# Second mixer's scan: clipped exponents, a triangle on the scores, paired gate SiLUs and a later norm root

## The chip, the cores and the metric

One core of one Trainium2 chip runs the whole program in a single launch. The metric is device time in microseconds (us), the median of several executions. All arithmetic is fp32; matmuls that need fp32 accuracy are done as three passes over split operands.

## The reference

Two blocks of two layers each on a sequence of 512 tokens with 1024 channels. The part that the change touches is the second block's second mixer, a state space mixer with 4 groups of 8 heads, cut here to what matters:

```
z, xbc, dt_raw = split(h @ w_in)
xbc = silu(causal_conv(xbc) + conv_b)
xs, b_in, c_in = split(xbc)
dt = softplus(dt_raw + dt_bias)
a_cs = cumsum(dt * a) within each chunk of 128 tokens
l_mat = exp(a_cs[t] - a_cs[s])          for s <= t, else 0
cb = c_in @ b_in^T                      scores of one chunk and group
y_diag = (cb * l_mat) @ (xs * dt)
states = b_in^T @ (xs * dt * exp(a_cs[end] - a_cs))
carry  = exp(a_cs[end]) * carry + states            over the chunks
y = y_diag + exp(a_cs) * (c_in @ carry) + xs * d
y = y * silu(z)
y = y * rsqrt(mean(y*y over the group's 512 channels) + eps) * norm_g
out = y @ w_out
```

## The kernel before

The program is written engine by engine: each engine (TensorE = PE, VectorE = DVE, ScalarE = ACT, GpSimd = POOL, SyncE = SP) has its own list of instructions in a fixed order, and they meet through counting semaphores. Nothing is scheduled by a planner; the order of the calls in `ssd_pe`, `ssd_act`, `ssd_dve`, `ssd_pool` and `ssd_sp` is the order of the work.

All projections stream their weights in slots of 256 columns: SP loads a slot (`w_raw`), ACT rounds it (`w_hi`, line 209), POOL takes the rest (`w_lo`, line 238, or line 2506 inside the scan, two instructions of 128x1024 a slot), and PE runs three matmuls per 128x128 tile (lines 248 to 250).

The scan runs 16 **slots**, v = 0 to 15, with group g = v // 4 and chunk c = v % 4. The work of one slot is spread over the engines:

- PE (`ssd_pe`): `z_half(v)`, 24 matmuls of the gate projection; `pre(v + 1)`, the transposes of x (line 2436) and the scores into `C_BANK` (line 2442); `main(v)`, per head the matmul of `lw` with `xdt` (line 2453) and, for c > 0, of `cdec` with the carried state `prev` (line 2455); then the chunk's state (line 2462). `main(v)` waits for `m_w` (DVE's product of slot v), `m_cd` (POOL's `cdec`) and `m_pv` (DVE's `states(v - 1)`).
- DVE (`ssd_dve`): `xdt` (line 2571), eight instructions of 128x128 for the exponents (line 2576), `outputs(v - 1)` (line 2548), the product of `lw` with the scores (line 2584), `states(v - 1)` (lines 2560 and 2563).
- ACT (`ssd_act`): `b_tok`, the exponentials of `cdec` (line 2486) and `lw` (line 2488), the SiLU of the gate `zT` (line 2491), and in odd slots the rounding of the next weight slot (`split_hi`). Going from one function to another costs an `ACT_TABLE_LOAD`.
- POOL (`ssd_pool`): `decay(v - 1)` of the carried state (line 2517), `xdec` (line 2528), the product for `cdec` (line 2534), and in even slots two instructions of `w_lo` (line 2506).
- SP (`ssd_sp`): `g_row` for slot v + 2 once slot v's exponents are taken (`m_dl`), the weight slots of the gate, and behind them those of `w_out`.

The norm of a finished group is laid into the next group's slots: the gating `gnorm_gate_dve` (line 2609, four of 128x512), squares on ACT (line 2615), column sums on PE (`gnorm_sums_pe`, line 2622, 8 matmuls at a time), root on ACT (`gnorm_root_act`, line 2628), reciprocal on DVE (`gnorm_rcp_dve`, line 2632), a spread over the partitions on PE (`gnorm_spread_pe`, line 2637), and the scaling on DVE (`gnorm_scale_dve`, line 2645, four of 128x512). Behind the scan `m_out_pe` starts the output projection while the last norms are finished.

The exponents before, with the mask (0 or a large negative number) as a second tensor from SBUF:

```
for k in range(8):
    op = dve.scalar_tensor_tensor(lw[v % 2][:, k, :], g_row[v % 2][:, k, :],
                                  mcols[:, M_CS, ...], upmask[:, :], ALU.subtract, ALU.add)
```

Of the kernel before, what the change touches and what calls it, by code (L numbers as in the profile page):

```python
# [26 lines left out]
P = 128  # L27
# [3 lines left out]
KD = D // P  # L31
# [75 lines left out]
def build(nc, t, out):  # L107

    ctx = ExitStack()
    with ctx:  # L110
# [2246 lines left out]
        def turn_steps_act(act):  # L2357
# [6 lines left out]
        (m_xt, m_cb, m_xd, m_dl, m_le, m_eg, m_w, m_bt, m_xe, m_cd, m_st, m_y, m_y1, m_yz, m_pd, m_pv) = (  # L2364
            sem("m_" + n) for n in "xt cb xd dl le eg w bt xe cd st y y1 yz pd pv".split())
# [47 lines left out]
        def ssd_pe(pe):  # L2413
# [50 lines left out]
            for v in range(16):  # L2464
                z_half(v)
                if v < 15:
                    pre(v + 1)
                main(v)
                if v >= 4 and v % 4 in (1, 2):
                    gnorm_sums_pe(pe, v // 4 - 1, v % 4 - 1)  # L2470
                if v >= 4 and v % 4 == 3:
                    gnorm_spread_pe(pe, v // 4 - 1)

        def ssd_act(act):
            for v in range(16):
# [63 lines left out]
        def ssd_dve(dve):  # L2539
# [25 lines left out]
            for v in range(16):  # L2565
# [9 lines left out]
                for k in range(8):  # L2575
                    op = dve.scalar_tensor_tensor(lw[v % 2][:, k, :], g_row[v % 2][:, k, :],  # L2576
                                                  mcols[:, M_CS, c * M_H + 8 * g + k:c * M_H + 8 * g + k + 1], upmask[:, :],
                                                  ALU.subtract, ALU.add)
                op.then_inc(m_dl, 1)
                if v:  # L2580
                    outputs(v - 1)
                dve.wait_ge(m_le, v + 1)
                dve.wait_ge(m_cb, v + 1)
                dve.tensor_tensor(lw[v % 2][:, :, :], lw[v % 2][:, :, :],
# [68 lines left out]
        def gnorm_act(act):  # L2653
# [363 lines left out]
```

## Time and profile before

| | us |
|---|---|
| three executions | 3088.41, 3088.75, 3091.66 (median 3088.75) |
| the profiled execution's span | 3086.1 |
| PE busy | 2914.6 (94%) |
| DVE busy | 1617.9 (52%) |
| POOL busy | 1212.1 (39%) |
| ACT busy | 1049.6 (34%) |

The span runs from the first to the last instruction of one profiled execution; its own device time is not listed apart from the three executions, which lie 2.3 to 5.6 us above that span. The profile has a page of totals, tables of busy time by stretch, a timeline of each engine with the idle time before a row and who ended it, and the mean duration of each group of instructions.

### The profile page before, as it was taken

To read this page: it belongs to the slowest core of one execution; us is meant where nothing else is said; L and a number is where in the kernel's file an instruction comes from. 1 tells how busy PE (TensorE), PEld (TensorE's weight loads), DVE (VectorE), ACT (ScalarE), POOL (GpSimd) and SP (SyncE) were. 2 spreads that over 40 slices of the span, in tenths; PEclk is the share of its full clock that TensorE was granted. 3 is DMA by queue.
4 is the path that set the end of the run, shared out by engine and by line. 5 is a ranking of instruction groups with operands and counts; after the bars stand their busy time and mean duration, and the time that the engine had idled before them with its cause. 6 is when DMAs were issued, how large, how long until landed. Compare 5 with 4: busy or idle time off the path is not lost.

```text
span 3086.1 us, 38851 instructions
## 1 busy us (share of the span) xinstructions
PE 2914.6 (94%) x14565; PEld 2374.3 (77%) x14565; DVE 1617.9 (52%) x2275; ACT 1049.6 (34%) x1327; POOL 1212.1 (39%) x556
## 2 busy tenths in 40 slices
PE   7999999999999999999998799999999988999998
PEld 6867886788877856788886677788878776778887
DVE  4435554776868146564556635555354766232224
ACT  4341122434332245333333222222235554232222
POOL 3433422344444410344443114444434544534443
PEclk9998998999999999999998779999999998999999
DMA  4320001334532320355533733655322322223322
GB/s 137 95 72 14 1 1 28 109 115 129 152 111 94 109 69 28 123 177 164 191 120 119 234 88 128 213 191 164 97 82 85 115 89 69 69 87 100 99 96 68
DMA packets 343961, 326.44 MB, mean 106 GB/s; under 512 B 28816, under 2 KB 320144, under 8 KB 343696
## 3 DMA queue, kind: packets, MB, share of 16 engines
q1 hardware_dynamic: 309760, 257.34, 26.9%
q10 hardware_dynamic: 34064, 67.18, 6.2%
q8 instruction: 97, 1.59, 0.2%
q14 instruction: 40, 0.33, 0.0%
HBM read 303.44 MB, written 21.04 MB: 105 GB/s over the span
## 4 chain that ended last, share of the span: by engine, by line
PE 72%; DVE 7%; issue 3%; ACT 2%; DMA 0%; POOL 0%; ACTq 0%; DVEq 0%; SPq 0%; POOLq 0%
PE bank L248 18%; PE bank L250 18%; PE bank L249 18%; PE bank L260 3%; PE bank L265 3%; PE bank L261 3%; PE bank L1328 2%; DVE lw L2576 1%; PE bank L1346 1%; PE bank L1336 1%; PE bank L1901 1%; PE bank L1896 1%; PE bank L2622 1%; PE bank L361 0%; DVE xt L404 0%
## 5 line engine op out<-in xcount | busy, mean ns | idle before, releaser
L238 POOL TENSOR_TENSOR w_lo<-w_raw,w_hi 128x1024 fp32r<-128x1024 f32 x400 | 1006.9, 2539 | 1446.0 <-ACT w_hi L209 1430.4
L248 PE MATMUL bank<-x_hi,w_hi 128*128 128x512 f32 x2032 | 799.5, 393 | 12.8 <-POOL w_lo L238 7.5
L250 PE MATMUL bank<-x_hi,w_lo 128*128 128x512 f32 x2032 | 793.3, 390 | 0.0
L249 PE MATMUL bank<-x_lo,w_hi 128*128 128x512 f32 x2032 | 793.1, 390 | 0.0
L209 ACT ACTIVATE w_hi<-w_raw 128x2048 fp32r<-128x2048 f32 x208 | 398.0, 1914 | 893.5 <-PE bank L250 787.5
L248 PEld LDWEIGHTS bank<-x_hi,w_hi 128*128 128x128 f32 x2032 | 383.7, 189 | 96.7 <-issue 14.9
L249 PEld LDWEIGHTS bank<-x_lo,w_hi 128*128 128x128 f32 x2032 | 383.5, 189 | 80.7 <-issue 1.6
L250 PEld LDWEIGHTS bank<-x_hi,w_lo 128*128 128x128 f32 x2032 | 382.9, 188 | 80.3
L248 PE MATMUL bank<-m_hi,w_hi 128*128 128x512 f32 x384 | 149.6, 390 | 0.0
L250 PE MATMUL bank<-m_hi,w_lo 128*128 128x512 f32 x384 | 149.4, 389 | 0.0
L249 PE MATMUL bank<-m_lo,w_hi 128*128 128x512 f32 x384 | 149.4, 389 | 0.0
L1210 DVE SCALAR_TENSOR_TENSOR y_gate<-bank,par,y_gate 128x511 f32<-128x511 f32 x88 | 66.0, 750 | 152.4 <-ACT y_gate L1144 150.7
L2209 DVE SCALAR_TENSOR_TENSOR h<-bank,mod,h 128x512 f32<-128x512 f32 (+1 forms) x64 | 47.4, 749 | 182.8 <-PE bank L250 165.7
L2188 DVE SCALAR_TENSOR_TENSOR m_r<-bank,m_r 128x512 f32<-128x512 f32 x64 | 43.8, 684 | 181.2 <-ACT m_r L2141 181.2
L1060 DVE SCALAR_TENSOR_TENSOR ada_acc<-ada_w,cond,ada_acc 128x1024 f32<-128x1024 f32 (+1 forms) x84 | 119.7, 1425 | 1.6
L2192 DVE TENSOR_TENSOR m_lo<-m_r,m_hi 128x512 fp32r<-128x512 f32 (+1 forms) x64 | 78.9, 1233 | 52.2 <-ACT m_hi L2143 52.2
L248 PE MATMUL bank<-act_hi,w_hi 128*128 128x512 f32 x264 | 103.2, 391 | 0.0
L250 PE MATMUL bank<-act_hi,w_lo 128*128 128x512 f32 x264 | 102.8, 389 | 0.0
L249 PE MATMUL bank<-act_lo,w_hi 128*128 128x512 f32 x264 | 102.7, 389 | 0.0
L260 PE MATMUL bank<-x_hi,w_hi 128*128 128x512 f32 x176 | 78.9, 448 | 18.3 <-ACT x_hi L373 7.0
L572 DVE SCALAR_TENSOR_TENSOR qkvz<-bank,par,qkvz 128x511 f32 (+2 forms) x72 | 53.8, 748 | 77.4 <-ACT qkvz L542 67.8
L836 POOL TENSOR_TENSOR X<-Rm,lev 128x512 f32<-128x512 f32 x56 | 70.3, 1270 | 54.4 <-PE bank L782 47.8
(437 smaller groups left out, 4762.1 us busy)
## 6 DMA issues: line engine op xcount, KB each, us to landing
w_raw<-in_mlp_w SPq DMA_DIRECT2D x128, 512.0 KB, 4.5
ada_w<-in_ada_w ACTq DMA_DIRECT2D x96, 512.0 KB, 4.9
w_raw<-in_f_w_up SPq DMA_DIRECT2D x88, 512.0 KB, 5.1
w_raw<-in_m_w_in SPq DMA_DIRECT2D x40, 512.0 KB, 4.7
w_raw<-in_a_w_in SPq DMA_DIRECT2D x32, 512.0 KB, 4.7
w_raw<-in_f_w_down SPq DMA_DIRECT2D x32, 512.0 KB, 4.0
w_raw<-in_w_kv SPq DMA_DIRECT2D x16, 512.0 KB, 4.3
w_raw<-in_s_w_glu SPq DMA_DIRECT2D x16, 512.0 KB, 5.3
```

The lines of the kernel that those rows point to most:

```text
L209: act.activation(w_hi[s][:, :], w_raw[s][:, :], ACT.Copy).then_inc(hi_done, 1)
L238: op = pool.tensor_tensor(w_lo[s][:, part], w_raw[s][:, part], w_hi[s][:, part].bitcast(F32), ALU.subtract)
L248: pe.matmul(dst, hi_l, hi_r, start=start, stop=False)
L249: pe.matmul(dst, hi_l, lo_r, start=False, stop=False)
L250: return pe.matmul(dst, lo_l, hi_r, start=False, stop=stop)
L260: pe.matmul(bank[o][:, :], w_hi[0][:, cols[o]], rhs_hi[:, k, :], start=(k == 0), stop=False)
L261: pe.matmul(bank[o][:, :], w_lo[0][:, cols[o]], rhs_hi[:, k, :], start=False, stop=False)
L265: mm = pe.matmul(bank[o][:, :], w_hi[0][:, cols[o]], rhs_lo[:, k, :], start=False, stop=(k == kt - 1))
L836: pool.tensor_tensor(X2[s][:, :, :], Rm[s][:, :, :], bc4(lev[:, l, :]), ALU.mult).then_inc(da_mask, 1)
L1060: dve.scalar_tensor_tensor(acc, ada_w[k][:, :, :], cond[:, k:k + 1], acc, ALU.mult, ALU.add).then_inc(ada_used, 1)
L1210: dve.scalar_tensor_tensor(y[:, s, d:T], bank[2 * s + o][:, 0:T - d], pcol("f_conv", i + (3 * 44 * f + 44 * (2 - d) + col + F_START[c] + s ...
L2192: dve.tensor_tensor(lo, m_r[:, o, :], m_hi[:, ds(2 * i + (2 * s + o), 1), :].bitcast(F32), ALU.subtract).then_inc(p_lo, 1)
```

## The change

1. The eight exponents of a slot no longer add the mask. They subtract and then clip at zero with `tensor_scalar`, which has one tensor operand. What the mask did is done on the scores: one new DVE instruction multiplies the 128x128 scores in PSUM by the 0/1 triangle `triu`, behind the waits for `m_le` and `m_cb`, and the product waits for it (`m_tri`).
2. ACT takes the gate's SiLU for slots v - 1 and v together, in odd slots.
3. The group norm is laid later: sums in the third and fourth slot of the next group (before: second and third), the root at the end of the first slot of the group after that (before: the fourth slot), the reciprocal in its second slot, the spread there ahead of `main(v)`, the scaling behind the states of that slot. For group 2 the root, the reciprocal and the spread move behind the scan, the spread between the first matmuls of the output projection.

```diff
--- before.py
+++ after.py
@@ -2361,8 +2361,8 @@
             act.dma_start(g_all, g_turn[:, :]).then_inc(m_gt, 16)
 
 
-        (m_xt, m_cb, m_xd, m_dl, m_le, m_eg, m_w, m_bt, m_xe, m_cd, m_st, m_y, m_y1, m_yz, m_pd, m_pv) = (
-            sem("m_" + n) for n in "xt cb xd dl le eg w bt xe cd st y y1 yz pd pv".split())
+        (m_xt, m_cb, m_xd, m_dl, m_le, m_eg, m_w, m_bt, m_xe, m_cd, m_st, m_y, m_y1, m_yz, m_pd, m_pv, m_tri) = (
+            sem("m_" + n) for n in "xt cb xd dl le eg w bt xe cd st y y1 yz pd pv tri".split())
         X_BANK, C_BANK, Y_BANK, N_BANK, S_BANK = bank[2], (bank[3], bank[7]), bank[4], bank[5], bank[6]
 
         def v8(x):
@@ -2465,11 +2465,11 @@
                 z_half(v)
                 if v < 15:
                     pre(v + 1)
+                if v >= 8 and v % 4 == 1:
+                    gnorm_spread_pe(pe, v // 4 - 2)
                 main(v)
-                if v >= 4 and v % 4 in (1, 2):
-                    gnorm_sums_pe(pe, v // 4 - 1, v % 4 - 1)
-                if v >= 4 and v % 4 == 3:
-                    gnorm_spread_pe(pe, v // 4 - 1)
+                if v >= 4 and v % 4 >= 2:
+                    gnorm_sums_pe(pe, v // 4 - 1, v % 4 - 2)
 
         def ssd_act(act):
             for v in range(16):
@@ -2486,16 +2486,17 @@
                     act.activation(cdec[e % 2][:, :, :], g_row[v % 2][:, :, :], ACT.Exp).then_inc(m_eg, 1)
                 act.wait_ge(m_dl, v + 1)
                 act.activation(lw[v % 2][:, :, :], lw[v % 2][:, :, :], ACT.Exp).then_inc(m_le, 1)
-                act.wait_ge(gemm_ready, 2 * z_slot(0) + v + 1)
-                ge(act, m_yz, v - 3)
-                act.activation(zT[:, v % 4, :], bank[v % 2][:, :], ACT.Silu).then_inc(bank_free, 1)
                 if v % 2:
+                    for z in (v - 1, v):
+                        act.wait_ge(gemm_ready, 2 * z_slot(0) + z + 1)
+                        ge(act, m_yz, z - 3)
+                        act.activation(zT[:, z % 4, :], bank[z % 2][:, :], ACT.Silu).then_inc(bank_free, 1)
                     n = z_slot(v // 2 + 2)
                     split_hi(act, n, n % 2, landed(n - n % 2))
                 if g and c in (1, 2):
                     gnorm_squares_act(act, g - 1, c - 1)
-                if g and c == 3:
-                    gnorm_root_act(act, g - 1)
+                if g >= 2 and c == 0:
+                    gnorm_root_act(act, g - 2)
 
         def pool_slot(pool, n):
 
@@ -2573,25 +2574,29 @@
                                   ALU.mult).then_inc(m_xd, 1)
                 dve.wait_ge(g_in[v % 2], 16 * (v // 2 + 1))
                 for k in range(8):
-                    op = dve.scalar_tensor_tensor(lw[v % 2][:, k, :], g_row[v % 2][:, k, :],
-                                                  mcols[:, M_CS, c * M_H + 8 * g + k:c * M_H + 8 * g + k + 1], upmask[:, :],
-                                                  ALU.subtract, ALU.add)
+                    op = dve.tensor_scalar(lw[v % 2][:, k, :], g_row[v % 2][:, k, :],
+                                           mcols[:, M_CS, c * M_H + 8 * g + k:c * M_H + 8 * g + k + 1], 0.0,
+                                           ALU.subtract, ALU.min)
                 op.then_inc(m_dl, 1)
                 if v:
                     outputs(v - 1)
+                if g >= 2 and c == 1:
+                    gnorm_rcp_dve(dve, g - 2)
                 dve.wait_ge(m_le, v + 1)
                 dve.wait_ge(m_cb, v + 1)
+                scores = C_BANK[v % 2][:, P:2 * P]
+                dve.tensor_tensor(scores, scores, triu[:, :], ALU.mult).then_inc(m_tri, 1)
+                dve.wait_ge(m_tri, v + 1)
                 dve.tensor_tensor(lw[v % 2][:, :, :], lw[v % 2][:, :, :],
                                   C_BANK[v % 2][:, P:2 * P].unsqueeze(1).to_broadcast([P, 8, P]), ALU.mult).then_inc(m_w, 1)
                 if v:
                     states(v - 1)
-                if v >= 4 and c == 0:
-                    if g >= 2:
-                        gnorm_scale_dve(dve, g - 2)
+                if g and c == 0:
                     gnorm_gate_dve(dve, g - 1)
-                if g and c == 3:
-                    gnorm_rcp_dve(dve, g - 1)
+                if g >= 2 and c == 1:
+                    gnorm_scale_dve(dve, g - 2)
             outputs(15)
+            gnorm_rcp_dve(dve, 2)
             gnorm_gate_dve(dve, 3)
             gnorm_scale_dve(dve, 2)
             gnorm_rcp_dve(dve, 3)
@@ -2651,6 +2656,7 @@
                 act.activation(y_hi[:, j, :], xbc[:, j, :], ACT.Copy).then_inc(hn_hi, 1)
 
         def gnorm_act(act):
+            gnorm_root_act(act, 2)
             act.wait_ge(gemm_ready, 2 * SLOTS["m_out"])
             gnorm_hi_act(act, 0, 8)
             gnorm_squares_act(act, 3, 0)
@@ -2703,10 +2709,13 @@
                         mm.then_inc(gemm_ready, 1)
             pe.wait_ge(lo_done, base + 1)
             pe.wait_ge(bank_free, 2 * base)
-            for k in range(4):
+            for k in range(2):
+                first_pair(0, k)
+            gnorm_spread_pe(pe, 2)
+            for k in range(2, 6):
                 first_pair(0, k)
             gnorm_sums_pe(pe, 3, 0)
-            for k in range(4, KD):
+            for k in range(6, KD):
                 first_pair(0, k)
             gnorm_sums_pe(pe, 3, 1)
             pe.wait_ge(lo_done, base + 2)
```

DVE around slots 8 and 9, from the reciprocal that stood at the end of slot 7. `xdt_164` and `lw_160` are the buffers of even slots, `xdt_165` and `lw_161` those of odd ones. Before:

```order
L2632 RECIPROCAL ncol<-ncol 128x4
L2571 TENSOR_TENSOR xdt_164<-bank,mcols 128x512
L2576 SCALAR_TENSOR_TENSOR lw_160<-g_row_158,mcols,upmask 128x128 x8
L2548 SCALAR_TENSOR_TENSOR xbc<-xbc,par,bank 128x128 x4
L2584 TENSOR_TENSOR lw_160<-lw_160,bank 128x1024
L2645 SCALAR_TENSOR_TENSOR xbc<-xbc,par,bank 128x512 x4
L2609 SCALAR_TENSOR_TENSOR xbc<-xbc,zT 128x512 x4
L2571 TENSOR_TENSOR xdt_165<-bank,mcols 128x512
```

After the change, the same two slots of DVE and the head of slot 10:

```order
L2572 TENSOR_TENSOR xdt_164<-bank,mcols 128x512
L2577 TENSOR_SCALAR lw_160<-g_row_158,mcols 128x128 x8
L2549 SCALAR_TENSOR_TENSOR xbc<-xbc,par,bank 128x128 x4
L2588 TENSOR_TENSOR bank<-bank,triu 128x128
L2590 TENSOR_TENSOR lw_160<-lw_160,bank 128x1024
L2614 SCALAR_TENSOR_TENSOR xbc<-xbc,zT 128x512 x4
L2572 TENSOR_TENSOR xdt_165<-bank,mcols 128x512
L2577 TENSOR_SCALAR lw_161<-g_row_159,mcols 128x128 x8
L2549 SCALAR_TENSOR_TENSOR xbc<-xbc,par,bank 128x128 x4
L2637 RECIPROCAL ncol<-ncol 128x4
L2588 TENSOR_TENSOR bank<-bank,triu 128x128
L2590 TENSOR_TENSOR lw_161<-lw_161,bank 128x1024
```

The reciprocal has left the place ahead of slot 8's `xdt` and stands in slot 9, and of the two sets of four in slot 8 only the gating is left; the scaling (line 2650) now comes behind slot 9's state copy.

PE at the end of slot 7, between `main(7)` and `z_half(8)`, as the difference of the two programs:

```order
 L2453 MATMUL bank<-lw_161,xdt_165 64x128
 L2455 MATMUL bank<-cdec_163,prev_169 64x128
-L2637 MATMUL bank<-ident,ncol 128x128 x4
+L2627 MATMUL bank<-ones,sq 128x1 x8
 L248 MATMUL bank<-x_hi,w_hi 128x512
```

The spread has left this place, and eight matmuls of sums have come to it from the slot before.

ACT in slots 9 and 10 after the change, from the table load of slot 9's exponentials:

```order
L2486 ACT_TABLE_LOAD
L2486 ACTIVATE cdec_162<-g_row_159 128x1024
L2488 ACTIVATE lw_161<-lw_161 128x1024
L2493 ACT_TABLE_LOAD
L2493 ACTIVATE zT<-bank 128x512 x2
L209 ACTIVATE w_hi<-w_raw 128x2048
L2620 ACTIVATE sq<-xbc 128x512 x2
L2481 ACTIVATE b_tok_171<-bank 128x128
```

Both SiLUs of the pair stand behind the exponential of slot 9, where each slot had one before, and the rounding and the squares come behind them as they did.

## Rows read from the trace of the kernel before

**Rows 1.** The page: the chain that ended last, by engine.

```profile
PE 72%; DVE 7%; issue 3%; ACT 2%; DMA 0%; POOL 0%; ACTq 0%; DVEq 0%; SPq 0%; POOLq 0%
```

**Rows 2.** Busy time by stretch: slots 1, 5, 7, 8, 9, 10, 13, 15, and 5 to 15.

```profile
core 0: us, PE busy (x) PEld busy (x) DVE busy (x) ACT busy (x) POOL busy (x), PEclk, DMA share, GB/s
2427.37:2436.62 9.25, 9.25 (x68) 7.46 (x66) 7.43 (x22) 7.04 (x8) 3.02 (x3) 1.00 0.53 170
2465.15:2480.68 15.53, 12.67 (x83) 10.59 (x82) 13.06 (x30) 12.48 (x15) 6.02 (x5) 0.89 0.33 103
2491.60:2502.53 10.93, 9.37 (x73) 7.97 (x73) 2.94 (x6) 6.35 (x7) 1.57 (x2) 1.00 0.47 141
2502.53:2514.73 12.20, 9.48 (x52) 7.42 (x51) 12.11 (x17) 1.34 (x2) 5.62 (x3) 0.87 0.13 44
2514.73:2531.63 16.90, 13.04 (x84) 10.94 (x82) 14.28 (x32) 13.59 (x15) 6.02 (x5) 0.89 0.32 94
2531.63:2542.58 10.95, 10.95 (x82) 9.13 (x82) 6.46 (x16) 6.38 (x9) 8.87 (x5) 1.00 0.14 52
2565.67:2586.80 21.13, 15.15 (x83) 12.52 (x82) 14.32 (x32) 13.28 (x15) 5.96 (x5) 0.82 0.37 125
2599.28:2610.20 10.92, 8.60 (x67) 7.10 (x66) 2.94 (x7) 6.36 (x8) 3.99 (x3) 1.00 0.01 3
2465.15:2610.20 145.05, 121.47 (x790) 100.45 (x788) 94.02 (x188) 80.82 (x90) 63.05 (x35) 0.92 0.24 77
```

**Rows 3.** Timeline of PE, slots 7 to 9: start, us, engine, line, [idle before <-releaser].

```profile
2497.18 0.60 PE L2436 MATMUL bank<-ident,xbc 128*128 128x128 f32 x4
...
2501.62 1.16 PE L2637 MATMUL bank<-ident,ncol 128*128 128x128 f32 x8 [1.56 <-DVE ncol L2632]
...
2511.74 1.98 PE L2453 MATMUL bank<-lw,xdt 128*64 128x128 f32 x16 [2.72 <-DVE lw L2584]
...
2525.54 0.70 PE L2453 MATMUL bank<-lw,xdt 128*64 128x128 f32 x4 [3.86 <-DVE prev L2560]
```

**Rows 4.** Timeline of DVE, slots 8 to 10.

```profile
2501.38 0.18 DVE L2632 RECIPROCAL ncol<-ncol 128x4 f32<-128x4 f32 x1 [7.99 <-ACT ncol L2628]
...
2502.10 7.24 DVE L2576 SCALAR_TENSOR_TENSOR lw<-g_row,mcols,upmask 128x128 f32<-128x128 f32 x8
...
2511.60 2.72 DVE L2645 SCALAR_TENSOR_TENSOR xbc<-xbc,par,bank 128x512 f32<-128x512 f32 x4
2514.24 2.49 DVE L2609 SCALAR_TENSOR_TENSOR xbc<-xbc,zT 128x512 f32<-128x512 f32 x4
...
2517.25 5.09 DVE L2576 SCALAR_TENSOR_TENSOR lw<-g_row,mcols,upmask 128x128 f32<-128x128 f32 x8
...
2523.46 1.22 DVE L2584 TENSOR_TENSOR lw<-lw,bank 128x1024 f32<-128x1024 f32 x1
2524.60 0.68 DVE L2560 COPY prev<-bank 128x512 f32<-128x512 f32 x1
...
2525.80 2.18 DVE L2576 SCALAR_TENSOR_TENSOR lw<-g_row,mcols,upmask 128x128 f32<-128x128 f32 x8
```

**Rows 5.** Groups of line 1395 by form (us, mean ns); L590 with POOL beside it.

```profile
L1395 DVE TENSOR_SCALAR prob<-prob,acol 128x512 f32<-128x512 f32 x16 | 7.7, 480 | 0.0
...
L1395 DVE TENSOR_SCALAR prob<-prob,acol 128x128 f32<-128x128 f32 x16 | 4.4, 278 | 0.0
...
2328.61 0.87 DVE L590 TENSOR_SCALAR mcols<-mcols 128x128 f32<-128x128 f32 x1 [1.75 <-ACT mcols L603]
...
2327.00 4.75 POOL L238 TENSOR_TENSOR w_lo<-w_raw,w_hi 128x1024 fp32r<-128x1024 f32 x2 [6.12 <-ACT w_hi L209]
```

**Rows 6.** Timeline of POOL in slot 8, and of ACT in slot 13.

```profile
2502.26 1.08 POOL L2528 TENSOR_TENSOR xdec<-xdt,mcols 128x512 f32<-128x512 f32 x1 [9.36 <-DVE xdt L2571]
2503.30 4.84 POOL L2506 TENSOR_TENSOR w_lo<-w_raw,w_hi 128x1024 fp32r<-128x1024 f32 x2
...
2580.82 1.91 ACT L209 ACTIVATE w_hi<-w_raw 128x2048 fp32r<-128x2048 f32 x1 [4.51 <-DMA w_raw<-in_m_w_out]
```

## Prediction

> **What bounds the kernel now.** I read the page first: of the span of 3086.1 us, 72% of the chain that ended last is PE and 7% DVE [rows 1]. So a change off PE pays only where PE waits for it. Next the stretches of the scan, slot by slot [rows 2]. The reader should compare three kinds of slot. Slot 1 is clean: 9.25 long, PE busy for all of it, clock 1.00. Slot 10 is clean with eight matmuls of sums in it: 10.95, so sums cost 1.70. Slots 8, 9 and 13 are not: 12.20, 16.90 and 21.13, with the granted clock at 0.87, 0.89 and 0.82, a mix of its two levels 1.2 and 2.4 GHz. PE waits and then runs part of the next work at the lower level: slot 9's busy time is 13.04 for the work that takes 10.95 in slot 10, so its wait costs 2.1 more in clock. PE's timeline names the waits [rows 3]: 1.56 for the reciprocal ahead of the spread in slot 7, 2.72 for DVE's product in slot 8, 3.86 for DVE's state in slot 9. DVE's timeline tells why DVE is late [rows 4]: it sat 7.99 for the root, so slot 8's exponents began at 2502.10, though the transposes for slot 8 had ended at 2497.8 [rows 3]. They then took 7.24 where the same eight take 2.18 in slot 10, because POOL's w_lo pair ran beside them [rows 6]. Scaling (2.72) and gating (2.49) stood between slot 8 and slot 9. Slots 12 and 13 repeat 8 and 9.
>
> **Clip instead of mask.** 128 instructions change form. Line 1395 is a tensor_scalar with a column operand, SBUF to SBUF: 278 ns for 128 columns and 480 for 512 [rows 5], that is 0.53 ns a column, two a cycle as the engine goes. The eight before take 2.18, 0.27 apart; I take 0.20 apart for the new ones, 1.65 for eight: 0.5 less a slot while POOL is quiet. Does one operand also free them of POOL? Line 590, 128x128 of the same kind, took 0.87 instead of 0.28 and ended at 2329.48, with POOL's first half (4.75 / 2) ending at 2329.4 [rows 5]. It waited for POOL. So blocked sets keep their length, 5.09 and 7.24 less about 0.1 to 0.3. The Trainium skill (SBUF — State Buffer, section Who interferes with whom) says the same against this part of the change: a tensor_scalar in a two-port mode takes the port pair that GpSimd uses, and the later one blocks fully. By that rule the trace agrees.
>
> **Triangle.** It has no row. From below it is the 0.28 of a 128-column instruction; from above the 0.68 of the 512-column copy out of PSUM [rows 4] and the 0.2 or so of a wait on the engine's own result, 0.86. I take 0.45, nearer the lower end by its size. It stands between exponential and product, on the path wherever DVE is late; it about eats the 0.5 of the clip. In clean slots PE's 9.25 covers both.
>
> **Paired SiLUs.** ACT loses about 14 table loads, but it is busy 6.35 of 10.93 in slot 7 [rows 2] and PE waits for none of them: I take 0 directly. Slots 4, 8 and 12 no longer hold ACT for the gating. The effect that matters is on POOL: `cdec` is ready sooner, so its product falls upon the exponents (below).
>
> **Norm laid later.** Worked through slots 7 to 15, against their lengths before.
>
> Slot 7: the wait (1.56) and the spread (2501.62 to the slot's end at 2502.53, 0.91) go, sums (1.70) come: 10.93 becomes 10.2.
>
> Slot 8: DVE starts at 2497.85 instead of 2501.49, 3.6 sooner. `main(8)` started at 2511.74 and could start at 2511.74 - 3.6 + 0.45 - 0.25 = 2508.3. PE was ready at 2511.74 - 2.72 = 2509.0, and is now at 2509.0 - 1.56 - 0.91 + 1.70 = 2508.25. The wait is gone, and with it the clock's loss: busy 9.48 at 0.87 is 8.3 at full clock. 12.20 becomes 8.4.
>
> Slot 9: from the gating's start (2514.24) to `main(9)` (2525.54) DVE's chain takes 11.3. It now follows the product of slot 8 at once, at 2508.2, and is 0.4 longer (triangle, reciprocal, shorter set): `main(9)` at 2519.9. PE is ready 8.3 after `main(8)`, at 2516.6. The gap of 3.3 holds the spread (0.9), which so costs nothing. Without sums: 9.25 + 3.3 = 12.5. I count no clock loss, since the spread splits the gap; its bound is the 2.1 of before.
>
> Slot 10 pays. Let M be the end of slot 9's state copy; `main(9)` starts at M + 0.35. The scaling now comes first: `xdt` at M + 2.6, exponents from M + 3.3. Before, they followed the copy at once and were done before `main(9)` ended and released POOL. Now `main(9)` ends at M + 2.3, and POOL runs decay and `xdec` (512 columns, 1.05 each as the 1.08 of [rows 6]) until M + 4.6, the `cdec` product (1024 columns, 2.4 as a half of w_lo's 4.75 [rows 5]) from M + 5.5, when ACT has rounded, squared, reloaded and exponentiated, and w_lo (2 x 2.4) behind it. Of the eight, one passes before M + 4.6 and five by M + 5.5; the seventh waits until M + 7.9, the eighth until M + 10.3. With outputs 1.2, exponential, triangle and product 1.7, state 0.7 and 0.35, `main(10)` starts at M + 14.4, and PE is ready at M + 0.35 + 9.25 = M + 9.6. That is a wait of nearly 5 and, at the clock loss between slots 8 (1.2) and 9 (2.1), 1.5: 10.95 becomes 17.4.
>
> Slots 11, 12, 13 repeat 7, 8, 9: 10.2, 8.4, 12.5. The 21.13 of slot 13 held another wait: its squares stood behind a rounding that waited for the first slot of w_out until 2580.82 [rows 6], which SP asks for only after slot 13's exponents. With the sums in slot 14 `main(13)` is free of it. But slot 14's exponentials stay behind it: the landing comes some 4 after `main(13)` (2525.54 + 50.94 = 2576.5 before), ACT's chain of rounding, squares, reload and two exponentials takes about 6.4 (its busy time in slot 15), triangle, product and state 2.7: `main(14)` 13.1 after `main(13)`, PE ready after 9.25. Wait 3.8, clock 1.5: 16.2. Slot 15: busy 8.60 less the spread, plus sums, plus about 1 for the root and the first y_hi behind it: 10.4.
>
> Slot 5 gives its sums (1.70) to slot 7, already counted there: 15.53 becomes 13.8; slot 6 stays 10.95.
>
> **Sum.** 13.8 + 10.95 + 10.2 + 8.4 + 12.5 + 17.4 + 10.2 + 8.4 + 12.5 + 16.2 + 10.4 = 131.0 against 145.05 [rows 2]: 14.1 less. Back go 0.6 in slots 3 to 5, where DVE is last and the triangle counts, 0.9 for group 2's spread, now between the output projection's first matmuls, and 1.0 because PE arrives there sooner while POOL's first y_lo still waits for w_lo. Result 11.6 less. The sum is made against the profiled execution; its span is 2.65 below the median, which I take as constant: 3088.75 - 11.6 = 3077.2.
>
> **Rivals.** *The eight slip through.* In slot 10 two instructions miss by 0.4. If ACT's `cdec` comes 0.4 later or the set is that much quicker, slot 10 is clean and 6.5 less; slot 14 stays. 18 less, 3070.7. For it: the margin is thin. Against it: six durations would all have to err one way. Chance 0.15.
>
> *Clipped exponents do not contend with POOL.* Then each set is 1.65 and every DVE wait in slots 3 to 14 goes: the slots sum to about 108, 37 less in 5 to 15; 2.5 in slots 3 and 4 come on top, 2 go back: about 37 less, 3051. The same page of the Trainium skill says that an instruction with one SBUF input outside the two-port modes does not contend. Against it stands line 590's 0.87 and the two columns a cycle [rows 5]. Chance 0.05.
>
> *More collisions.* Slot 6 is the next in danger: its set must be over before `main(5)` releases POOL, by my count at M + 2.3 against M + 2.4. If it is caught there it costs the 6.5 of slot 10: 5.1 less, 3083.6, just no difference. Chance 0.12.
>
> *Slower.* DVE becomes the bound through POOL: with `cdec` early in every slot, sets are caught in slots 2 and 6 too, and one more of the eight behind w_lo (2.4) in 10 and 14. Place: the even slots, where POOL's list is 9.3 long against PE's 9.25 to 10.95. 13 + 4.8 come on top of the forecast: 6.2 more, 3095. It decides once a set starts less than 1.65 before the previous `main` ends. For it: 7.24 and 5.09 against 2.18. Against it: slots 1, 2 and 6 have no scaling in front of their `xdt`. Chance 0.07.
>
> **How the numbers follow.** Forecast 0.61, the rivals 0.15, 0.05, 0.12, 0.07. The forecast's own spread: triangle 0.28 to 0.86 over some seven slots on the path, -1.2 to +2.9; clock 0 to 2.1 in slots 9, 10, 13, 14, +-3; together about 3071 to 3083. The range adds the slip at one end and the one collision at the other: 3069.5 to 3084.5, leaving out the third and the last rival and the edges. A measurement tells 0.2%, 6.2 us, from nothing. Faster: 0.61 x 0.95 + 0.15 + 0.05 = 0.78; slower 0.07 and a little from the others, 0.08; the rest 0.14.
>
> **What would show it.** PE in slots 7 and 11 without a wait, `main(8)` and `main(12)` waiting under 0.5 and slot 8 at 8 to 9 long; the reciprocal's idle time gone from 7.99; slot 10 longer than before, its last two clipped instructions over 2 us each, its wait on the state about 5; tensor_scalar of line 2577 at 275 to 280 ns where POOL is quiet. The forecast is wrong if that set is never blocked, if slot 8 still waits over 2, or if slot 6 grows by over 3.

## Result and profile after

The changed kernel takes 3069.66 us (median of four executions, 3068.18 to 3070.39) against 3089.54 for the kernel before on the same chip (3088.41 to 3091.66): ratio 0.9933, 95% interval 0.9919 to 0.9946. That is 19.9 us less by the medians and 0.67% less by the ratio. The profiled span is 3067.7, 18.4 less than before. The forecast was 11.6 less, with a range from 19.3 less to 4.3 less.

The page's chain still has 72% PE and 7% DVE, so the kind of bound has not changed [rows 1]:

```profile
PE 72%; DVE 7%; issue 3%; ACT 2%; POOL 1%; DMA 0%; ACTq 0%; DVEq 0%; SPq 0%; POOLq 0%
```

Busy time by stretch, slots 1, 5, 7, 8, 9, 10, 13, 14, 15 and then 5 to 15, to set beside [rows 2]:

```profile
core 0: us, PE busy (x) PEld busy (x) DVE busy (x) ACT busy (x) POOL busy (x), PEclk, DMA share, GB/s
2427.31:2436.91 9.60, 9.28 (x67) 7.45 (x66) 9.25 (x25) 6.03 (x7) 2.83 (x3) 1.00 0.53 159
2465.10:2478.61 13.51, 10.87 (x67) 9.02 (x66) 11.67 (x29) 7.53 (x9) 3.80 (x3) 0.87 0.37 118
2489.87:2500.06 10.19, 10.19 (x82) 8.87 (x81) 6.78 (x12) 8.26 (x9) 5.40 (x3) 1.00 0.43 154
2500.06:2508.06 8.00, 8.00 (x51) 6.46 (x51) 7.87 (x14) 4.07 (x5) 2.86 (x2) 1.00 0.23 68
2508.06:2519.65 11.59, 10.39 (x75) 8.43 (x74) 11.55 (x23) 7.11 (x9) 3.81 (x3) 1.00 0.43 126
2519.65:2530.89 11.24, 11.24 (x83) 9.22 (x81) 10.77 (x22) 4.51 (x6) 9.68 (x6) 1.00 0.17 59
2549.08:2560.66 11.58, 10.37 (x75) 8.43 (x74) 11.54 (x23) 4.59 (x6) 3.80 (x3) 1.00 0.38 112
2560.66:2578.83 18.17, 13.65 (x83) 11.13 (x81) 13.04 (x29) 7.03 (x8) 9.66 (x6) 0.81 0.34 108
2578.83:2589.33 10.50, 9.54 (x75) 8.08 (x74) 3.87 (x9) 9.02 (x11) 4.70 (x2) 1.00 0.13 43
2465.10:2589.33 124.23, 113.71 (x782) 94.17 (x780) 100.42 (x200) 67.25 (x77) 61.74 (x34) 0.96 0.28 90
```

The scan's slots 5 to 15 took 145.05 and now take 124.23: 20.8 less. Slots 8 and 9 have PE at the full clock, and slot 10, which the forecast made the expensive one, is clean: PE is busy for all of its 11.24. Only slots 5 and 14 still show the clock between its levels. PE's timeline in slots 8, 9, 10 and 14, beside [rows 3]:

```profile
2506.47 1.09 PE L2453 MATMUL bank<-lw,xdt 128*64 128x128 f32 x16
...
2514.81 1.16 PE L2642 MATMUL bank<-ident,ncol 128*128 128x128 f32 x8
2517.17 0.45 PE L2453 MATMUL bank<-lw,xdt 128*64 128x128 f32 x4 [1.20 <-DVE prev L2561]
...
2526.27 0.45 PE L2453 MATMUL bank<-lw,xdt 128*64 128x128 f32 x4
...
2571.89 0.70 PE L2453 MATMUL bank<-lw,xdt 128*64 128x128 f32 x4 [4.51 <-DVE prev L2564]
```

`main(8)` and `main(10)` start with no wait, `main(9)` waits 1.20 where it waited 3.86, and the spread stands in the gap in front of it. DVE's timeline in slots 8 to 10, beside [rows 4]:

```profile
2496.69 6.72 DVE L2577 TENSOR_SCALAR lw<-g_row,mcols 128x128 f32<-128x128 f32 x8
...
2504.53 0.30 DVE L2588 TENSOR_TENSOR bank<-bank,triu 128x128 f32<-128x128 f32 x1
2504.86 1.22 DVE L2590 TENSOR_TENSOR lw<-lw,bank 128x1024 f32<-128x1024 f32 x1
...
2509.01 4.62 DVE L2577 TENSOR_SCALAR lw<-g_row,mcols 128x128 f32<-128x128 f32 x8
...
2514.59 0.17 DVE L2637 RECIPROCAL ncol<-ncol 128x4 f32<-128x4 f32 x1
...
2516.23 0.68 DVE L2561 COPY prev<-bank 128x512 f32<-128x512 f32 x1
2516.83 2.71 DVE L2650 SCALAR_TENSOR_TENSOR xbc<-xbc,par,bank 128x512 f32<-128x512 f32 x4
...
2520.06 2.48 DVE L2577 TENSOR_SCALAR lw<-g_row,mcols 128x128 f32<-128x128 f32 x8
```

The reciprocal no longer waits (7.99 before). The sets of slots 8 and 9 are still blocked, 6.72 and 4.62 against 7.24 and 5.09. The set of slot 10 took 2.48, not the 7 that the forecast gave it. POOL's timeline says why (slots 9 and 10), and ACT's gives the exponential that POOL's `cdec` product waits for:

```profile
2509.17 1.04 POOL L2529 TENSOR_TENSOR xdec<-xdt,mcols 128x512 f32<-128x512 f32 x1 [6.25 <-DVE xdt L2572]
2510.18 2.39 POOL L2535 TENSOR_TENSOR cdec<-cdec,xbc 128x1024 f32<-128x1024 f32 x1
...
2520.24 1.04 POOL L2529 TENSOR_TENSOR xdec<-xdt,mcols 128x512 f32<-128x512 f32 x1
2522.57 2.40 POOL L2535 TENSOR_TENSOR cdec<-cdec,xbc 128x1024 f32<-128x1024 f32 x1 [1.29 <-ACT cdec L2486]
```

```profile
2521.43 1.06 ACT L2486 ACTIVATE cdec<-g_row 128x1024 f32<-128x1024 f32 x1
...
2563.02 1.92 ACT L209 ACTIVATE w_hi<-w_raw 128x2048 fp32r<-128x2048 f32 x1 [4.88 <-DMA w_raw<-in_m_w_out]
```

In slot 10 the set ends at 2522.54 and the product begins at 2522.57, 0.03 later. In slot 9 the product begins at 2510.18, 1.17 into the set, and the set waits for it. The last row is why slot 14 is long: the rounding waits 4.88 for w_out.

### The profile page after: what moved, and what is told of

The parts are those of the page before. It is cut to its first block, busy times and chain, and to the rows that moved or that the text cites. A ratio compares the mean times of both kernels' runs of the same rounds, so it can differ in the third digit from the quotient of the medians.

```text
span 3067.7 us, 38853 instructions
## 1 busy us (share of the span) xinstructions
PE 2910.0 (95%) x14565; PEld 2372.6 (77%) x14565; DVE 1625.9 (53%) x2291; ACT 1031.2 (34%) x1313; POOL 1210.7 (39%) x556
## 4 chain that ended last, share of the span: by engine, by line
PE 72%; DVE 7%; issue 3%; ACT 2%; POOL 1%; DMA 0%; ACTq 0%; DVEq 0%; SPq 0%; POOLq 0%
PE bank L248 18%; PE bank L250 18%; PE bank L249 18%; PE bank L260 3%; PE bank L265 3%; PE bank L261 3%; PE bank L1328 2%; PE bank L1346 1%; DVE lw L2577 1%; PE bank L1336 1%; PE bank L1901 1%; PE bank L1896 1%; PE bank L361 0%; DVE xt L404 0%; PE bank L1354 0%
```

## Experiments

Twelve further kernels were run. The table gives slot lengths, from one start of `z_half` on PE to the next in each profiled execution; medians are of the timed executions. The kernel before had medians of 3088.66 (the first four), 3089.05 (`norm_clip` to `extra1`) and 3089.07 (the last four) beside them. The intervals are some 4 us to either side, so where two kernels differ by less than that, the slots of their profiles carry the reading and the medians only go along with it.

| kernel | median | ratio (95%) | slot 5 | 8 | 9 | 10 | 13 | 14 |
|---|---|---|---|---|---|---|---|---|
| before | 3089.54 | 1 | 15.53 | 12.20 | 16.90 | 10.95 | 21.13 | 12.48 |
| changed | 3069.66 | 0.9933 (0.9919 to 0.9946) | 13.51 | 8.00 | 11.59 | 11.24 | 11.58 | 18.17 |
| norm_only | 3072.99 | 0.9944 (0.9930 to 0.9958) | 13.66 | 8.00 | 10.42 | 16.99 | 10.38 | 18.38 |
| clip_only | 3078.67 | 0.9963 (0.9949 to 0.9976) | 11.88 | 12.08 | 13.10 | 10.93 | 18.43 | 12.27 |
| silu_only | 3091.84 | 1.0007 (0.9998 to 1.0016) | 15.82 | 11.20 | 18.07 | 10.92 | 20.77 | 13.73 |
| mask_back | 3069.69 | 0.9935 (0.9922 to 0.9949) | 12.07 | 8.01 | 11.90 | 11.24 | 11.91 | 17.67 |
| norm_clip | 3068.44 | 0.9932 (0.9919 to 0.9946) | 9.78 | 8.02 | 10.49 | 16.66 | 10.47 | 18.22 |
| cdec_late | 3063.12 | 0.9919 (0.9906 to 0.9933) | 10.81 | 8.00 | 10.48 | 12.12 | 10.48 | 18.52 |
| wout_early | 3063.66 | 0.9912 (0.9899 to 0.9926) | 13.49 | 8.00 | 11.58 | 11.26 | 11.59 | 11.26 |
| extra1 | 3067.48 | 0.9931 (0.9915 to 0.9946) | 13.57 | 8.00 | 11.59 | 11.23 | 11.59 | 18.35 |
| extra2 | 3073.50 | 0.9946 (0.9931 to 0.9961) | 13.46 | 8.00 | 11.59 | 15.17 | 11.59 | 17.57 |
| no_tri | 3068.66 | 0.9935 (0.9920 to 0.9950) | 12.84 | 8.00 | 10.93 | 11.24 | 10.93 | 17.81 |
| late_wout | 3058.82 | 0.9899 (0.9884 to 0.9914) | 10.82 | 8.01 | 10.47 | 12.14 | 10.49 | 12.13 |
| late_wout_mask | 3063.06 | 0.9919 (0.9906 to 0.9933) | 12.60 | 8.00 | 11.13 | 12.56 | 10.71 | 12.57 |

### The three parts, one at a time

**norm_only**: the kernel before with the norm laid later and nothing else.

```diff
-                if v >= 4 and v % 4 in (1, 2):
-                    gnorm_sums_pe(pe, v // 4 - 1, v % 4 - 1)
+                if v >= 4 and v % 4 >= 2:
+                    gnorm_sums_pe(pe, v // 4 - 1, v % 4 - 2)
...
-                if g and c == 3:
-                    gnorm_root_act(act, g - 1)
+                if g >= 2 and c == 0:
+                    gnorm_root_act(act, g - 2)
...
```

> The kernel before with the later norm alone (mask and single SiLUs kept). Theory A (the norm's order carries the gain; the clip pays only by letting slot 10's set of eight end before POOL's cdec product): slots 7, 8, 9 shorten as in the changed kernel (about 10.3, 8.1, 11), but the masked set of slot 10 is caught by POOL and slot 10 is 16 to 20 long; 12 to 15 us faster than before. Theory B (the clip itself carries about half of the gain by its shorter sets): 8 to 11 us faster, slot 10 at 11.

**clip_only**: the kernel before with clip and triangle alone.

```diff
-                    op = dve.scalar_tensor_tensor(...upmask[:, :], ALU.subtract, ALU.add)
+                    op = dve.tensor_scalar(...0.0, ALU.subtract, ALU.min)
...
+                dve.tensor_tensor(scores, scores, triu[:, :], ALU.mult).then_inc(m_tri, 1)
+                dve.wait_ge(m_tri, v + 1)
```

> The kernel before with clip and triangle alone. Theory A: 0 to 3 us faster, since slots 7 to 9 and 13 keep their waits. Theory B: 8 to 10 us faster.

**silu_only**: the kernel before with paired SiLUs alone.

```diff
-                act.activation(zT[:, v % 4, :], bank[v % 2][:, :], ACT.Silu).then_inc(bank_free, 1)
                 if v % 2:
+                    for z in (v - 1, v):
...
+                        act.activation(zT[:, z % 4, :], bank[z % 2][:, :], ACT.Silu).then_inc(bank_free, 1)
```

> The kernel before with the paired SiLUs alone. Theory A: within 1 us of before, though ACT loses about 14 table loads. Rival (ACT is on the path in the scan): 3 us or more faster.

**mask_back**: the changed kernel with masked exponents and no triangle, that is, the edit of `clip_only` undone.

```diff
-                    op = dve.tensor_scalar(...0.0, ALU.subtract, ALU.min)
+                    op = dve.scalar_tensor_tensor(...upmask[:, :], ALU.subtract, ALU.add)
...
-                dve.tensor_tensor(scores, scores, triu[:, :], ALU.mult).then_inc(m_tri, 1)
-                dve.wait_ge(m_tri, v + 1)
```

> The changed kernel with the masked exponents back and no triangle. Theory A: slot 10's set takes over 4.5 instead of 2.5, slot 10 is 15 to 18 long instead of 11.2, the rest within 1 us: 4 to 7 us slower than the changed kernel, 13 to 16 faster than before. Theory B: 9 to 10 us slower than the changed kernel, spread over all slots. If clip and triangle just cancel and the margin in slot 10 does not decide: within 1 us of the changed kernel.

The norm alone gives 15.7 of the 19.9, and in it slot 10 does what the forecast said: 16.99 long. The sum of the parts is not the whole. By slots 1 to 15 of the profiles, norm alone has -16.5, clip alone -11.0 and SiLU alone +1.0, which would make -26.5, and the changed kernel has -20.8. (By the medians it is -15.7, -10.0, +3.2 and -19.9; the interval of `silu_only` spans no change.) Putting the mask back costs nothing (3069.69 against 3069.66; slots 1 to 15 are 0.5 shorter), as the third expectation had it, though clipping alone gains 10.0. So the theory that clip pays only by rescuing slot 10 fell twice: the masked set slips through slot 10 too, and clip pays most in slots 5, 9 and 13 of a kernel whose norm has not moved. The rows of slot 9, DVE and then POOL of `clip_only`:

```profile
2517.80 2.47 DVE L2576 TENSOR_SCALAR lw<-g_row,mcols 128x128 f32<-128x128 f32 x8
```

```profile
2520.06 2.47 POOL L2534 TENSOR_TENSOR cdec<-cdec,xbc 128x1024 f32<-128x1024 f32 x1 [1.06 <-ACT cdec L2486]
```

The clipped set is out at 2520.27, while POOL's product starts at 2520.06: the last of the eight was already running. The masked set of before, from 2517.25, needed 0.27 apiece, was still at work when the same product came at 2519.51, and took 5.09 [rows 4]. Slot 10 of `norm_only`, DVE and POOL:

```profile
2520.29 7.21 DVE L2576 SCALAR_TENSOR_TENSOR lw<-g_row,mcols,upmask 128x128 f32<-128x128 f32 x8
```

```profile
2522.51 2.48 POOL L2534 TENSOR_TENSOR cdec<-cdec,xbc 128x1024 f32<-128x1024 f32 x1 [0.97 <-ACT cdec L2486]
2524.94 4.78 POOL L2506 TENSOR_TENSOR w_lo<-w_raw,w_hi 128x1024 fp32r<-128x1024 f32 x2
```

Here the product starts 2.22 into a masked set. In `mask_back` the masked set slips through the same slot. DVE and POOL:

```profile
2519.72 3.00 DVE L2577 SCALAR_TENSOR_TENSOR lw<-g_row,mcols,upmask 128x128 f32<-128x128 f32 x8
```

```profile
2522.57 2.42 POOL L2535 TENSOR_TENSOR cdec<-cdec,xbc 128x1024 f32<-128x1024 f32 x1 [1.57 <-ACT cdec L2486]
```

Slot 9's set, which ACT and DVE both start from, ends at 2513.63 in `mask_back` and in the changed kernel alike. ACT's way from there to the product takes the same time (2522.57 in both), but the set of slot 10 starts 0.34 earlier (2519.72 against 2520.06), because the triangle no longer stands on DVE's way to it. So it starts 2.85 ahead of the product, and its last instruction is already running: what the mask costs here, leaving the triangle out gives back. In every case the question is whether POOL's product starts before the set's last instruction does. That made a third theory: the parts meet in the moment at which `cdec` becomes ready. It says that with single SiLUs the clipped sets of 5 and 9 slip and that of 10 is caught, and that moving `cdec` alone frees them all.

### The moment of `cdec`

**norm_clip**: the changed kernel with one SiLU a slot.

```diff
+                act.activation(zT[:, v % 4, :], bank[v % 2][:, :], ACT.Silu).then_inc(bank_free, 1)
                 if v % 2:
-                    for z in (v - 1, v):
```

> The changed kernel with single SiLUs again (clip and later norm kept). Theory C, formed after the first four runs: what decides is whether POOL's cdec product comes while DVE's set of eight runs; the paired SiLU brings it about 2 us sooner and so spends what the clip gives. Then slots 5, 9 and 13 fall from 13.5, 11.6, 11.6 to about 10.2 to 10.7 each and slot 10 is caught (15 to 17): 1 to 3 us either side of the changed kernel. Rival (paired SiLU does nothing, as the run of it alone read): every slot as in the changed kernel, total within 1 us.

Both came: slots 5 and 9 fell to 9.78 and 10.49, slot 10 rose to 16.66. DVE and POOL in its slots 9 and 10:

```profile
2506.02 2.46 DVE L2576 TENSOR_SCALAR lw<-g_row,mcols 128x128 f32<-128x128 f32 x8
...
2516.13 6.76 DVE L2576 TENSOR_SCALAR lw<-g_row,mcols 128x128 f32<-128x128 f32 x8
```

```profile
2509.86 2.39 POOL L2534 TENSOR_TENSOR cdec<-cdec,xbc 128x1024 f32<-128x1024 f32 x1 [2.63 <-ACT cdec L2486]
...
2518.09 2.40 POOL L2534 TENSOR_TENSOR cdec<-cdec,xbc 128x1024 f32<-128x1024 f32 x1 [0.75 <-ACT cdec L2486]
```

So the pairing of SiLUs acts twice, in opposite directions. In odd slots ACT's exponential for `cdec` no longer stands behind the even slot's SiLU and comes during the set (product 1.17 into it, against 3.84 here). In even slots it stands behind two SiLUs, which take 0.5 more than the one here, and POOL's idle time ahead of the product grows from 0.75 to 1.29. The first costs slots 5, 9 and 13 5.9 together, the second saves slot 10 5.4; the medians of the two kernels are the same within their intervals.

**cdec_late**: the changed kernel with ACT's exponential of `cdec` behind the one of `lw`.

```diff
+                act.wait_ge(m_dl, v + 1)
+                act.activation(lw[v % 2][:, :, :], lw[v % 2][:, :, :], ACT.Exp).then_inc(m_le, 1)
                 if c:
...
                     act.activation(cdec[e % 2][:, :, :], g_row[v % 2][:, :, :], ACT.Exp).then_inc(m_eg, 1)
-                act.wait_ge(m_dl, v + 1)
-                act.activation(lw[v % 2][:, :, :], lw[v % 2][:, :, :], ACT.Exp).then_inc(m_le, 1)
```

> The changed kernel with ACT's exponential for cdec behind the one for lw, so that POOL's product can't meet the set of its own slot. Theory C: the sets of slots 1, 5, 9, 13 take 2.5 to 2.8 instead of 4.6, PE's waits there fall by 1 to 2 each (less what the later cdec costs main, up to 0.9), 2 to 5 us faster than the changed kernel. Rival (sets are slow for w_lo and xdec, or cdec becomes the last wait): no gain, or 1 to 4 us slower.

It is 6.5 faster than the changed kernel by the medians and 4.8 by slots 1 to 15; expected were 2 to 5. The intervals of the two ratios overlap, so the slots are the firmer figure. The product cannot meet the set now, since its input waits for the set: in slot 9 the set is 2.46 long and POOL's product comes at 2508.35, 4.58 after the set's start:

```profile
2503.77 2.46 DVE L2577 TENSOR_SCALAR lw<-g_row,mcols 128x128 f32<-128x128 f32 x8
```

```profile
2508.35 2.37 POOL L2535 TENSOR_TENSOR cdec<-cdec,xbc 128x1024 f32<-128x1024 f32 x1 [3.38 <-ACT cdec L2488]
```

Its price is 0.9 in slot 10 (12.12 against 11.24), where `main(10)` now waits 0.81. The profile names no releaser for that wait; `main(10)` starts at 2520.84, 0.11 after POOL's `cdec` product has ended (2520.73).

### How wide slot 10's margin is

**extra1** and **extra2**: one or two more clipped exponents, into buffers that nothing reads, ahead of slot 10's eight.

```diff
+                if v == 10:
+                    for spare in (upmask, g_turn)[:2]:
+                        dve.tensor_scalar(spare[:, :], g_row[v % 2][:, 0, :], ..., 0.0, ALU.subtract, ALU.min)
```

(`extra1` has `[:1]`.)

> The changed kernel with a ninth clipped exponent in slot 10 alone, written to a spare tile. The margin theory of the prediction: the set ended at 2522.54 and POOL's cdec product began at 2522.57, so one more instruction is caught: the set takes over 4.5 instead of 2.5 and slot 10 is 13 to 14 long instead of 11.2. Rival (the margin isn't what it seems): slot 10 grows by 0.2 at most.

> The changed kernel with two more clipped exponents ahead of slot 10's eight (into spare buffers, results not used). One more changed nothing. If the set of slot 10 has a margin of 0.2 to 0.4 before POOL's cdec product, the last instruction now waits for POOL, the set is 4.5 or longer and slot 10 is 12.5 to 15 in place of 11.24, 1 to 4 more in all. If the margin is larger, slot 10 stays at 11.2 and the time is that of the changed kernel.

One more changed nothing, so the 0.03 between set and product isn't the margin. Two more cost 3.9 in slot 10. DVE and POOL of `extra1`, and then of `extra2`:

```profile
2519.02 2.46 DVE L2582 TENSOR_SCALAR lw<-g_row,mcols 128x128 f32<-128x128 f32 x8
```

```profile
2521.31 2.44 POOL L2535 TENSOR_TENSOR cdec<-cdec,xbc 128x1024 f32<-128x1024 f32 x1 [1.29 <-ACT cdec L2486]
```

```profile
2522.94 1.08 DVE L2578 TENSOR_SCALAR g_turn<-g_row,mcols 128x128 f32<-128x128 f32 x1
2523.94 3.79 DVE L2582 TENSOR_SCALAR lw<-g_row,mcols 128x128 f32<-128x128 f32 x8
```

```profile
2525.23 2.42 POOL L2535 TENSOR_TENSOR cdec<-cdec,xbc 128x1024 f32<-128x1024 f32 x1 [1.29 <-ACT cdec L2486]
```

In `extra1` the set ends at 2521.48, 0.17 after POOL's product has started: an instruction that was already running was not held up. In `extra2` the set ends at 2527.73, 0.08 after POOL's product ends (2525.23 + 2.42 = 2527.65). The set begins anew when `xdec` lets go, and 1.29 of POOL's idle time are room for six instructions at 0.2 and one already running; the changed kernel needs six, `extra1` seven, `extra2` eight. So the slip has a margin of one instruction, about 0.2. By the single instructions in the traces, the last of the set starts 0.31 before POOL's product in the changed kernel, 0.10 before it in `extra1` and 0.08 after it in `extra2`, where it takes 2.42 instead of 0.28. The slot grew by 3.9, of which 2.25 are `main(10)`'s wait; the rest, 1.7, is busy time at a granted clock of 0.89.

### Slot 14, the triangle, and all together

**wout_early**: the changed kernel, with SP asking for the first two slots of w_out ahead of the last two `g_row`.

```diff
+            for i in range(2):
+                sp_slot(sp, SLOTS["m_out"] + i, halves(rows_k(t["m2_w_out"][0]), i, 0, KD, KD * i))
             g_load(14)
             g_load(15)
...
```

(What is left out makes the output projection's own loads start behind these two.)

> The changed kernel with the loads of w_out's first two slots ahead of g_row 14 and 15 in SP's queue. Theory: slot 14's wait of 4.5 and its clock loss come from ACT standing behind that landing (4.88 idle before the rounding); slot 14 falls from 18.2 to 11 to 12.5, 4 to 7 us faster than the changed kernel. Rival (slot 14 is late for its own set or for POOL): 0 to 2 us.

Slot 14 fell from 18.17 to 11.26, the time by 6.0 by the medians, and no other of the table moved by over 0.02; the rounding that waited 4.88 now follows the SiLUs without a wait:

```profile
2560.06 1.92 ACT L215 ACTIVATE w_hi<-w_raw 128x2048 fp32r<-128x2048 f32 x1
```

**no_tri**: the changed kernel without the triangle's product, so that its results lack the causal mask.

```diff
-                dve.tensor_tensor(scores, scores, triu[:, :], ALU.mult).then_inc(m_tri, 1)
-                dve.wait_ge(m_tri, v + 1)
```

> The changed kernel without the product of the scores with the triangle; this leaves the triangle out of the computation. By the profile it costs 0.30 and a wait of 0.03, so slots 3, 4, 5, 9, 13 and 14, where DVE comes last, are 0.3 each shorter: 1.5 to 2 less. If the semaphore's round trip costs more than the profile shows, 0.6 each: 3 to 4 less. If the earlier product shifts POOL or ACT against the sets, a slot moves by 1 or more either way.

Slots 5, 9 and 13 are 0.67, 0.66 and 0.65 shorter, twice what the triangle's row shows (0.30 and a wait of 0.03), while the medians are 1.0 apart, within their intervals, and slots 1 to 15 together 2.6. The traces show where the 0.66 of slot 9 comes from: two triangles stand on DVE's way to `main(9)`. Without slot 8's, for which PE doesn't wait itself, the set of slot 9 starts 0.62 into the slot instead of 0.95; without slot 9's own, `main(9)` starts 8.45 into it instead of 9.11. In slot 5 one triangle shortens the wait (2.64 to 2.30), and the other 0.33 is busy time at a lower clock (10.87 to 10.54). So the triangle costs its 0.33 each time, as the first expectation said, and not the 0.6 of the second; what that expectation missed is that two of them fall into slots 9 and 13.

**late_wout** puts `cdec_late` and `wout_early` together; **late_wout_mask** is that kernel with mask for clip and without the triangle. Their edits are the ones above.

> Both single changes on the changed kernel together: the exponential of cdec behind the one of lw, and the first two slots of w_out asked for ahead of g_row 14. Theory C (what DVE pays depends on when POOL's cdec product comes against the exponents) and the account of slot 14 (a wait for w_out) are independent if they hold: slots 5, 9 and 13 are 10.8, 10.5 and 10.5 long as with the late exponential alone, slot 14 is 11 to 12.5 in place of 18.2 to 18.5, together 12 to 14 less than the changed kernel: 3056 to 3059. Rival: with w_out early, slot 14's cdec product falls on its set or on that of slot 15, slot 14 is 14 or longer and the time 3059 to 3063.

> The kernel of late_wout with the masked exponents and without the triangle. If clipping is worth something only where POOL is in reach of a set, it is worth nearly nothing here: eight exponents cost 0.5 more, the triangle's 0.33 goes, so 0 to 1 more than late_wout, and slots 5, 9 and 13 are 10.5 to 11.3. Rival: the longer masked sets are caught once more in slots 5, 9 or 10, each 1.5 to 3 longer, 3 to 8 more in all.

`late_wout` came as its first theory said, and is the fastest kernel of the study: 3058.82 against 3089.07, a ratio of 0.9899 (0.9884 to 0.9914), which lies wholly below that of the changed kernel. Its stretches, slots 5, 9, 10, 14 and then 5 to 15:

```profile
2466.73:2477.55 10.82, 9.31 (x68) 7.47 (x66) 10.02 (x29) 7.00 (x8) 3.81 (x3) 1.00 0.36 105
...
2507.00:2517.47 10.47, 10.16 (x75) 8.35 (x74) 9.40 (x23) 7.10 (x9) 3.81 (x3) 1.00 0.34 104
2517.47:2529.61 12.14, 11.28 (x83) 9.22 (x81) 11.74 (x21) 4.31 (x6) 8.74 (x6) 1.00 0.24 85
...
2558.27:2570.40 12.13, 11.29 (x83) 9.22 (x81) 11.72 (x21) 4.30 (x6) 8.74 (x6) 1.00 0.00 0
2466.73:2581.64 114.91, 109.43 (x781) 90.53 (x780) 99.97 (x200) 68.10 (x78) 62.35 (x35) 1.00 0.30 97
```

All of slots 5 to 15 run at the full clock, in 114.91. With the mask it is 4.2 slower by the medians and 4.8 by slots 5 to 15, so the expectation that clip is worth nearly nothing there missed. The reason is neither of the two theories. The masked set of slot 9 is only 0.5 longer, and no `cdec` product meets it:

```profile
2506.70 2.97 DVE L2585 SCALAR_TENSOR_TENSOR lw<-g_row,mcols,upmask 128x128 f32<-128x128 f32 x8
```

```profile
2511.79 2.35 POOL L2543 TENSOR_TENSOR cdec<-cdec,xbc 128x1024 f32<-128x1024 f32 x1 [3.84 <-ACT cdec L2496]
```

But `cdec` now stands behind the set, so the half microsecond goes through `lw`'s exponential, `cdec`'s and POOL's product to PE in nearly every slot: `main(10)` waits 1.27 for `cdec` where it waited 0.86. The triangle, which clip pays in exchange, isn't on that path. The largest part is slot 5, 12.60 against 10.82: its wait is 2.03 instead of 1.50, and behind it PE is busy 10.57 instead of 9.31, at a granted clock of 0.89. That 1.3 of clock neither expectation had.

## Why the prediction was off

The direction was right, and the mechanisms that it names are real, but the collision that it charged most for did not happen in this kernel: one term of its sum, 6.2 of 6.8, carried the error. Slot by slot, forecast and measured: 13.8 and 13.51; 10.95 and 11.26; 10.2 and 10.19; 8.4 and 8.00; 12.5 and 11.59; **17.4 and 11.24**; 10.2 and 10.19; 8.4 and 8.00; 12.5 and 11.58; **16.2 and 18.17**; 10.4 and 10.50. Forecast 131.0, measured 124.23.

- **The reciprocal's wait and `main(8)`**: right. Slots 7 and 11 match to 0.01, the idle time of 7.99 is gone, and slot 8 is 8.00.
- **The step that failed** is "Of the eight, one passes before M + 4.6 and five by M + 5.5; the seventh waits until M + 7.9, the eighth until M + 10.3." M is 2516.91. Measured from M, `main(9)` and `xdt` came as forecast, POOL's decay at M + 2.33 (2.3) and `xdt` at M + 2.55 (2.6). But `xdec` was over at M + 4.37 instead of 4.6, since it follows the decay at once, and the `cdec` product started at M + 5.66 instead of 5.5. Between them lie 1.29 where the forecast had 0.9. The six that were left need 1.2, and the set was out at M + 5.63, 0.03 before the product. (An instruction already running isn't held up, as `extra1` shows; the forecast didn't grant that, and here it wasn't needed.) So the whole 6.2 hung on 0.4, and my chance for it (0.15, because "six durations would all have to err one way") was too low: it took two errors, of 0.23 and 0.16. By the forecast's own signs, slot 10's two instructions over 2 us and its wait of about 5 are missing. The rival "the eight slip through" named the place, the 0.4 and, with 3070.7, nearly the time; that the time came so near is partly luck, since slots 9 and 13 (1.8 less) and slot 14 (2.0 more) missed by as much in opposite directions.
- That the collision is real was shown three times: slot 10 is 16.99 with the norm alone, 16.66 with norm and clip, 15.17 with two instructions more.
- **Paired SiLUs**: nothing directly, as forecast. That `cdec` is ready sooner holds for odd slots alone. In even slots the second SiLU makes it later, and that is what lifted the gap of slot 10 from 0.75 to 1.29. The forecast took `cdec`'s time from ACT's order but didn't weigh the pairing on both sides.
- **Clip instead of mask**: the quiet set takes 1.65 as forecast. Beside POOL the clipped sets are 6.72 and 4.62 against 7.24 and 5.09, a little more off than the 0.1 to 0.3 granted. By the Trainium skill (SBUF — State Buffer, section Who interferes with whom) a tensor_scalar in its two-port mode and a GpSimd instruction exclude each other for a whole instruction; the trace agrees: an instruction of line 2577 takes 277 ns by the median and 636 by the mean of the scan, and the one in slot 9 that meets POOL's product of 2.39 takes 2.43. What the forecast left out of this term is that a quicker set can slip in front of POOL in the odd slots: in the kernel before that is worth 10 us, in slots 5, 9 and 13.
- **Triangle**: 0.33 by its row and by `no_tri`, within the bounds, below the 0.45 taken.
- **Slots 9 and 13**: 0.9 less than forecast each. DVE's chain from the gating's start to `main(9)` took 11.17 instead of 11.7 (the set 0.47 shorter), and the gating starts 0.47 ahead of `main(8)`, not with it. That they lose no clock was right.
- **Slot 14**: mechanism right, size off. w_out's rounding began 4.84 after `main(13)` (forecast some 4), ACT's chain behind it took 6.43 (6.4), so the wait is 4.51 instead of 3.8. The clock took some 2.4 instead of 1.5: 18.17 less the wait is 13.66 for what takes 11.24 in slot 10. `wout_early` takes both away, 6.9 in that slot.
- **What goes back**: nothing in slots 1 to 4 together (forecast 0.6). Behind the scan 2.5 (20.9 earlier at its end, 18.4 at the program's) against 1.9 forecast, with the first `y_lo` waited for 3.42 instead of 2.02.

## What to carry to other kernels

Where the instructions of two engines shut each other out, as DVE's exponents and POOL's products do here, a set of short instructions costs either its own time or that plus whole instructions of the other engine, and which of the two is decided by the moment when the other's input is ready. So cost such a place as two cases with the gap in microseconds between them, give the nearer one no more weight than the gap deserves, and follow each edit on a third engine (here ACT's order) to that moment. Better than winning such a race is to take it away: ordering `cdec` behind the set gave 6.5 us by the medians (4.8 by the slots), where clip and paired SiLUs together add 3.3 (4.4 by the slots) to the norm's move. And the gains of single edits at such a place don't add: by the medians, clip is worth 10.0, 4.6, 0.0 and 4.2 us in four surroundings (before, `norm_only`, `mask_back`, `late_wout_mask`), and 11.0, 3.8, -0.5 and 5.5 by slots 1 to 15.

## What was not expected of the hardware

- Not every DVE instruction was held up by POOL. In slot 10 the product of line 2590, which reads the scores from PSUM, ran from 2524.00 to 2525.22, beside POOL's product (to 2524.97) and w_lo behind it, in 1.22, as in slot 8 with POOL idle.
- Waits of the same size can cost clock or not. In slot 5 `main(5)` waits 2.64 in the changed kernel, and the slot is 13.51 at a granted clock of 0.87, between the levels of 1.2 and 2.4 GHz. In `mask_back` it waits 2.79, and the slot is 12.07 at 1.00. In `late_wout_mask` a shorter wait of 2.03 goes with 10.57 busy at 0.89. Ahead of the wait the first two differ in slot 3, where `main(3)` waits 1.48 in `mask_back` and 0.89 in the changed kernel; but `silu_only` waits 1.50 there and still has slot 5 at 0.89, so that alone doesn't decide it. Why one loses 1.6 of busy time and the other nothing stays open, and a forecast of such a clock term should keep both values.

```profile
2465.88:2477.95 12.07, 9.28 (x67) 7.46 (x66) 11.98 (x27) 5.62 (x6) 3.89 (x3) 1.00 0.36 115
```

This row is slot 5 of `mask_back`, to set beside slot 5 of the changed kernel above: PE is busy 9.28 here and 10.87 there, for the same matmuls.
